# Reordering the RWKV units of a hybrid diffusion step: squares of both head halves first, preparation a half level later

## What is computed

```python
def step(s, inp):
    r_t, d_t, k_t, v_t, kk_t, kka_t = inp
    sa = jnp.einsum('bhij,bhj->bhi', s, kk_t)
    s = s * d_t[:, :, None, :] - sa[..., None] * kka_t[:, :, None, :] + v_t[..., None] * k_t[:, :, None, :]
    y = jnp.einsum('bhij,bhj->bhi', s, r_t)
    return s, y
```

## Time and profile before

| | |
|---|---|
| median of three runs | 2578.04 us (2569.5 to 2580.0) |
| the profiled execution | 2574.44 us, of which the span from first to last instruction is 2572.6 us |
| mean granted TensorE clock | 0.937 of full speed |
| PE busy | 2314.1 us (90%) |
| DVE busy | 1782.1 us (69%) |
| ACT busy | 470.7 us (18%) |
| POOL busy | 949.4 us (37%) |

### The profile page before, as it was taken

How to read it: one execution, slowest core, us unless ns; L and a number is a source line. 1 busy time by engine, 2 the same in 40 slices (tenths; PEclk the granted TensorE clock), 3 DMA queues, 4 the chain that set the end, 5 groups by cost and what they waited for, 6 DMA issues and landing times.

```text
span 2572.6 us, 42533 instructions
## 1 busy us (share of the span) xinstructions
PE 2314.1 (90%) x17474; PEld 1609.3 (63%) x17474; DVE 1782.1 (69%) x3492; ACT 470.7 (18%) x994; POOL 949.4 (37%) x774
## 2 busy tenths in 40 slices
PE   7999969787888878998899699999999999999997
PEld 3555528576666763344488677776776677775664
DVE  1211263266788865775898876899899898876767
ACT  2111214134334421001212111000001000000101
POOL 0000000001445540443620005767665667664653
PEclk9999969888989988998999589999999999999998
DMA  8341130311556652876972029999999999999997
GB/s 314 134 164 62 65 123 3 123 42 57 180 190 225 217 192 86 316 264 244 353 296 81 18 89 364 374 387 387 409 405 349 409 409 406 395 396 411 409 409 301
DMA packets 163931, 646.94 MB, mean 251 GB/s; under 512 B 21062, under 2 KB 21958, under 8 KB 158298
## 3 DMA queue, kind: packets, MB, share of 16 engines
q0 software_dynamic: 110592, 402.70, 41.6%
q1 hardware_dynamic: 53146, 241.52, 24.4%
HBM read 635.50 MB, written 8.65 MB: 250 GB/s over the span
## 4 chain that ended last, share of the span: by engine, by line
PE 62%; DVE 15%; DMA 9%; issue 8%; ACT 4%; POOL 2%; another core or an unknown queue 1%; SPq 0%; DVEq 0%; POOLq 0%; ACTq 0%
PE ps L1106 9%; PE ps L1117 9%; DMA arena<-in_peer_v,arena 8%; PE ps L611 6%; PE ps L1128 5%; PE ps L1082 4%; POOL arena L2299 2%; PE ps L1022 2%; PE ps L989 2%; PE ps L1032 2%; DVE arena L2122 2%; PE ps L1047 2%; PE ps L615 2%; PE ps L870 1%; PE ps L800 1%
## 5 line engine op out<-in xcount | busy, mean ns | idle before, releaser
L1117 PE MATMUL ps<-arena 128*128 128x512 f32 x1024 | 466.6, 599 | 24.5 <-DVE arena L2161 24.5
L1106 PE MATMUL ps<-arena 128*128 128x256 f32 x2048 | 476.9, 387 | 0.0
L2299 POOL DMA_INDIRECT arena<-in_peer_u,arena x256 | 335.5, 1310 | 352.5 <-DVE arena L1911 191.3
L1106 PEld LDWEIGHTS ps<-arena 128*128 128x128 f32 x2048 | 390.0, 194 | 68.6 <-issue 19.9
L2299 POOL DMA_INDIRECT arena<-in_peer_v,arena x256 | 301.1, 1176 | 203.3 <-DVE arena L2122 137.5
L2122 DVE SCALAR_TENSOR_TENSOR arena<-arena 128x1024 f32<-128x1024 f32 x252 | 315.8, 1283 | 83.2 <-DMA arena<-in_peer_v,arena 78.6
L2287 POOL DMA_INDIRECT arena<-in_peer_u,arena x128 | 167.7, 1310 | 522.8 <-DVE arena L1911 300.0
L1117 PEld LDWEIGHTS ps<-arena 128*128 128x128 f32 x1024 | 194.5, 192 | 224.6 <-issue 217.6
L2117 DVE SCALAR_TENSOR_TENSOR arena<-arena 128x1024 bf16<-128x1024 f32 x256 | 303.6, 1222 | 34.4 <-DMA arena<-in_peer_u,arena 27.9
L1128 PEld LDWEIGHTS ps<-arena 128*128 128x128 bf16 x3072 | 205.6, 157 | 69.5 <-issue 46.7
L1128 PE MATMUL ps<-arena 128*128 128x32 bf16 x3072 | 208.2, 242 | 23.2 <-DVE arena L2154 22.2
(11 more groups left out here) (365 smaller groups left out, 3253.9 us busy)
## 6 DMA issues: line engine op xcount, KB each, us to landing
arena<-in_uT SPq DMA_DIRECT2D x128, 512.0 KB
arena<-in_peer_v SPq DMA_DIRECT2D x128, 512.0 KB
arena<-in_w_ada SPq DMA_DIRECT2D x12, 2048.0 KB, 21.4
arena<-in_peer_wq SPq DMA_DIRECT2D x12, 2048.0 KB, 9.6
arena<-in_w_in SPq DMA_DIRECT2D x6, 2048.0 KB, 8.3
arena<-in_w_out SPq DMA_DIRECT2D x4, 2048.0 KB, 8.9
arena<-in_peer_u,arena POOLq DMA_INDIRECT x384
arena<-in_peer_v,arena POOLq DMA_INDIRECT x384
```

What stands on the lines that cost most here:

```text
L1106: m = pe.matmul(ps[:, 4 + i % 2, 0:ND], us[i % UB][:, k, :], hTd[:, k, :], start=(k == 0), stop=(k == KD - 1))
L1117: m = pe.matmul(ps[:, 2 * r + c, :], sgel[:, i % SBUFS, P * r:P * r + P], vs[i % VB][:, 512 * c:512 * c + 512], start=(i == 0), stop=(i == ...
L2299: pool.indirect_dma_start(gring[:, n % RING, :], None, a[("peer_u", "peer_v")[e]][0], bass.IndirectOffsetOnAxis(ap=ids[:, t, m:m + 1], axi ...
```

## The change

Three things change, all in the RWKV units:

- PE issues `squares(0, 1)` before the 16 value products instead of behind them.
- ACT copies the value products (L1328 before) behind the copies of both halves' squares of level 0, instead of ahead of them.
- The tables of the preparation move. On PE the low-rank products go from place 1 to 2 and the cumulative sums from 3 to 4; totals and transposes stay at 7 to 11. On ACT the two sigmoids go from 1 and 2 to 3 and 4, the three exponentials from 4, 5, 5 to 5, 6, 6; the rest stays. On DVE every group goes one place later.

```diff
-PREP_PE = (1, 3, 7, 8, 9, 10, 11)
-PREP_ACT = {1: 1, 2: 1, 4: 1, 5: 2, 7: 1, 8: 1, 9: 1, 10: 1, 11: 1}
-PREP_DVE = {2: 2, 3: 2, 4: 3, 5: 2, 6: 1}
+PREP_PE = (2, 4, 7, 8, 9, 10, 11)
+PREP_ACT = {3: 1, 4: 1, 5: 1, 6: 2, 7: 1, 8: 1, 9: 1, 10: 1, 11: 1}
+PREP_DVE = {3: 2, 4: 2, 5: 3, 6: 2, 7: 1}
...
                 squares(0, 0).then_inc(S("r_lv"), 1)
                 pe.wait_ge(S("r_mask"), 6 * n + 4)
+                squares(0, 1).then_inc(S("r_lv"), 1)
                 for h in range(HEADS):
                     for c in range(2):
                         r = slice(64 * c, 64 * c + 64)
                         m = pe.matmul(ps[r, 0, 64 * h:64 * h + 64], lm[r, h, 2, :], rkv[r, t, 2, 64 * h:64 * h + 64], start=True, stop=True)
                 m.then_inc(S("r_s2"), 1)
-                squares(0, 1).then_inc(S("r_lv"), 1)
...
-                act.wait_ge(S("r_s2"), n + 1)
-                own.do(A(zz[:, :, 1, :, :].rearrange("p u i j -> p u (i j)"), ps[:, 0, :].rearrange("p (u x) -> p u x", x=P), ACT.Copy), S("r_x0"))
                 ahead = prepare(n + 1 if chained else len(UNITS))
                 for l in range(LEVELS):
                     for g in range(2):
...
                             own.do(A(solT[:, 2 * g:2 * g + 2, :, :].rearrange("p u i j -> p (u i j)"), ps[:, 1 + 3 * g, 0:4 * CH], ACT.Copy), S("r_lvx"))
+                        if 2 * l + g == 1:
+                            act.wait_ge(S("r_s2"), n + 1)
+                            own.do(A(zz[:, :, 1, :, :].rearrange("p u i j -> p u (i j)"), ps[:, 0, :].rearrange("p (u x) -> p u x", x=P), ACT.Copy), S("r_x0"))
                         for _ in range(PREP_ACT.get(2 * l + g, 0)):
                             next(ahead)
```

## The result

The changed kernel took 2613.38 us (median of 4 runs, 2589.1 to 2615.9) against 2575.2 us for the kernel before on the same chips: ratio 1.0122, 95% interval 1.0078 to 1.0166. It is slower by about 31 us (20 to 43 by the interval; the medians differ by 38). The profiled execution took 2614.54 us, 40 us more than the one before. The forecast of slower holds. The time lies on the upper bound of the range (2583 to 2613), 16 us above the 2597 forecast.

A forecast was written before the change was run, and what follows sets the result against it. PE was taken to bound the kernel, with the whole difference carried. Stops of +16.2 us and clock falls of +5.3 gave +21.5 on 2574.44, 2595.9; with the median's offset 2597 us, range 2583 to 2613.

The forecast's parts named there:

- PE and the stages behind set the end, the difference is carried whole: All units: PE carries most of the last-ending chain, later stages only follow, so the whole difference reaches the end.
- Level 0: Value products, squares and low-rank products up to L708: no cost or gain, except 0.35 us gained each in units 1 and 9.
- Sigmoids: Ahead of the cumulative sums L708: PE stands 2.8 us for the second sigmoid; L708 starts at 11.11 in unit 0.
- Exponentials: Ahead of L714: new PE stop of 1.8 us until the third exponential at 19.2; the 0.94 us stop at (3,1) goes.
- First transposes, units 0, 2 and 3: L724 at 21.8 us in units 0 and 2, losing 4.05 and 3.8 us; unit 3 hides its delay behind DVE, cost nothing.
- First transposes, units 4 to 8: L724 in the five gathered units: 1.8 us lost each, 9.0 us together; unit 5 at 22.94 against 21.15.
- The sum of the stops: All units: 4.05 + 3.8 + 9.0 - 0.7 = +16.2 us before any charge for the clock.
- The clock: Behind the first transposes: a fall to 1.2 GHz costing 1.5 us in every second of seven units, +5.3 us (0 to 10.5).
- my first rival: Clock falls after both stops in all seven units (21 us), or instruction shortage adds 7 us: 2605 to 2613 us; chance 0.14.
- rival 2: Gathered units absorb their share, only units 0 and 2 pay: +7.2 us, 2582 to 2585 us; chance 0.20.
- rival 3: Second sigmoid done before (2,0) ends, so no new stop and today's stops go: -13.1 us, 2561 us; chance 0.05.
- The Trainium skill's figure for a table switch: The two loads in PE's way: by the page's drain 19 us more, 2616 us; given no chance of its own.

The follow-up runs named there:

- The order alone: Changed kernel's order of squares and value products with the preparation tables of the kernel before: 2518.97 us, B + 2.7, ratio 1.0017.
- B: The kernel before, unchanged, on the same chip as the run compared: 2516.3 us for four runs, 2571.1 for the next four, 2572.6 for the last four.
- the first four: Runs on one chip (B 2516.3 us): old tables in the changed kernel 2518.97, new tables in the kernel before 2559.69, sigmoids one place earlier 2538.74, useless products added 2542.84.
- the fillers: Changed kernel plus products nothing reads, five ahead of L708's wait, three ahead of L714's: 2542.84 us, on another chip 2593.59, ratio 1.0102 to B both times.
- the tables alone: Kernel before, in its old order, with the changed kernel's preparation tables: 2559.69 us, B + 43, ratio 1.0176.

## Why the prediction came out as it did

- *PE and the stages behind set the end, the difference is carried whole*: held. From the last mask of unit 0 (392.0 and 393.75) to the chunk steps of unit 9 (961.56 and 1003.01) the two traces drift apart by 39.7 us, of 40.1 in the whole span.
- *Level 0*: held. The order alone gave B + 2.7 us with the old tables, less than the 5.6 us by which L703 waits there, a wait that the new tables avoid. In unit 1 the last products come 0.47 us sooner after the mask (14.88 instead of 15.35), for 0.35 forecast.
- *Sigmoids*: held to the decimal in unit 0. 2.8 us forecast, 2.79 in the trace; L708 at 11.11 forecast, at 11.14 after the mask.
- *Exponentials*: the stop was right (1.8 and 1.83), its place was not: L714 came at 20.92, not 19.25. From L708 to L714 it took 9.78 us instead of the 8.14 laid out. No wait lies between; the products there were at the lower clock (L708 1.55 us instead of 1.12).
- *First transposes, units 0, 2 and 3*: unit 0 at 23.80 instead of 21.8, 6.05 us later than before and not 4.05; unit 2 at 598.62 - 574.41 = 24.2 instead of 21.8. Unit 3 hid its delay: its wait of 5.85 us is gone and L724 came 24.3 us after the mask against 23.7.

```profile
574.41 0.33 PE L835 MATMUL ps<-arena 64*64 64x64 f32 x4 [0.22 <-DVE arena L1721]
...
598.62 1.11 PE L724 MATMUL ps<-arena 128*128 128x128 f32 x4 [0.57 <-DVE arena L1710]
```

- *First transposes, units 4 to 8*: this failed. 1.8 us each were forecast. Unit 4 came 1.6 us later after the mask, units 5 to 8 came 9.8, 6.1, 9.7 and 6.2 us later (unit 5 at 30.9 us instead of 21.15). The layout had PE at L708 from 8.33 us on; in unit 5 it got there at 14.25, in unit 6 at 9.74. Unit 5's value products ran at the lower clock (1.71 us for 28 of them, 1.10 for all 32 in unit 0), and in (2,0) PE lacked instructions several times, 0.93 us once. The stops of 2.1 to 3.1 us came on top.

```profile
729.20 0.33 PE L835 MATMUL ps<-arena 64*64 64x64 f32 x4 [1.17 <-DVE arena L1721]
...
741.29 0.35 PE L870 MATMUL ps<-arena 64*64 64x64 f32 x1 [0.93 <-issue]
...
745.59 2.08 PE L708 MATMUL ps<-arena 128*128 128x512 f32 x2 [2.14 <-ACT arena L1247]
...
760.11 1.12 PE L724 MATMUL ps<-arena 128*128 128x128 f32 x4 [0.42 <-DVE arena L1710]
```

- *The sum of the stops*, 16.2 us: the four named waits grew by 17.7, but this is agreement by luck. PE's idle time from unit 0 to unit 9 grew by only 3.3 us, since waits for DVE that the forecast had left as they were became shorter. The layout also missed most of what units 5 to 8 lost. Units 3 and 9 were 3.7 and 3.1 us shorter than before. Between the two runs on the chip of the first four, PE's idle time did grow, by 19.8 us.
- *The clock*, 7 x 1.5 / 2 = 5.3 us: this is the term that was mis-sized. The same products took 36.4 us longer in this trace and 20.4 us longer in the pair of runs on one chip, and the fillers gave back 12 to 22 us of device time. I had priced one fall behind each second unit's transposes. In the trace the first transposes run at the lower clock in all eight preparing units (1.11 us instead of 0.66), and behind the stop of 2.8 us the cumulative sums are at the lower clock, in whole or in part, in seven of them. In unit 0 that is 1.64 us between L708 and L714, about 0.4 from there to L724 and 0.7 from L724 to L885 (5.33 instead of 4.65), 2.7 us in all; 7 x 3 = 21 us was the price that my first rival named, with a chance of 0.14. So the direction and the mechanism were the forecast's, and the time was that rival's (2605 to 2613). The step that failed was to take the frequency from a stop of 0.9 us, for which the earlier trace rows show one fall in two units and the trace before one in five (only unit 5 took more than 4.65 us from L724 to L885), for stops of 2.8 and 1.8 us.
- *Absorbed in the gathered units* (rival 2): no, they paid most. The trace shows 1.6 to 3.1 us of stop at L708 in them, and units 4 to 8 together are 31.8 us longer. How this divides between the clock and PE's shortage of instructions I could not separate; that stays open. On the chip of the first four runs, where the traces show no such gaps in the loop, the tables alone cost B + 43, not less.
- *Faster* (rival 3): its condition, a second sigmoid done before (2,0) ends, is what the run with the sigmoids one place earlier came near to, and the stop at L708 went in most units; the kernel was still slower than before.
- The Trainium skill's figure for a table switch (ScalarE: Activation LUTs, section What ACT_TABLE_LOAD costs: 1.28 us of load and a drain of 1.38 us) again has only its first half here: the load started at 401.64 and the sigmoid at 402.93.

## What to carry to other kernels

When a step is moved on one engine's queue, move it on the others by what it waits for, not by the same number of places: here the sigmoids went two places on ACT and their consumer one on PE, and a consumer at the same place as its producer waits for the copies and the table load in front of it. Give a table load a place of its own, by an activation of one column issued where the engine is idle; that alone made the kernel before 0.5 to 0.8% faster. And price a new stop of TensorE above its own length: between the two runs on one chip the longer products cost as much (20.4 us) as the idle time (19.8 us), and in the first trace of the changed kernel nearly the whole loss was longer products. Last, check the forecast's sum against the whole idle time, and not only against the waits that it names.

## What the hardware showed that I had not expected

- Stops of 2.8 and 1.8 us let the granted clock fall to its lower level in almost every unit, while stops of 0.9 us did so only now and then; filling 2.4 and 1.4 us of them with useless products brought back 12 to 22 us.
- The same kernel before took 2516 us on one chip and 2571 to 2575 on the others, a spread of 2%, larger than the effect studied; its ratios to the variants were alike (fillers 1.0102 on both).
